# One layer of attention and mLSTM on one core: the first weight block is rounded by VectorE, and the products of zeros around the first transposes are set anew

## What is computed

```
h = rms_norm(x, pre_norm_g[l])
proj = jnp.einsum('bsd,dc->bsc', h, w_in[l])
aq, ak, av, az, mq, mk, mv, mo, mz, mi, mf = split_columns(proj)
...
y = jnp.einsum('bsc,cd->bsd', jnp.concatenate([ya, ym], axis=-1), w_out[l])
x = x + rms_norm(y, post_norm_g[l])
```

## Time and profile before

| | |
|---|---|
| median of 3 runs | 326.0 us (325.98 to 326.64) |
| the profiled execution, its own time | 326.21 us |
| its span, first to last instruction | 324.1 us |
| TensorE busy | 316.8 us, 98% of the span |
| VectorE, ScalarE, GpSimd busy | 224.6, 167.2, 88.4 us |
| granted TensorE clock, mean | 0.995 |

### The profile page before, as it was taken

The page is one execution under the profiler, slowest core; times in us unless marked ns, Lnnn a source line. Parts: engine busy times, 40 slices in busy tenths (PEclk is TensorE's granted clock), DMA queues, the critical chain, the costliest instruction groups (busy, mean ns, idle before and its releaser), DMA issues.

```text
span 324.1 us, 5056 instructions
## 1 busy us (share of the span) xinstructions
PE 316.8 (98%) x1638; PEld 262.0 (81%) x1638; DVE 224.6 (69%) x533; ACT 167.2 (52%) x335; POOL 88.4 (27%) x113
## 2 busy tenths in 40 slices
PE   7999999999999999999999999999999999999993
PEld 5887788888888888888888888778888888888882
DVE  2444999857998579976897557675477776765534
ACT  3538662598345434664257442375556976442211
POOL 8101002205440222002220025591721975001000
PEclk9999999999999999999999999999999999999998
DMA  7931553843735581145823332210120366010111
GB/s 222 303 85 48 135 168 81 157 141 97 137 73 137 136 168 36 32 133 135 138 66 103 93 97 68 77 58 31 60 70 2 119 198 270 2 65 2 65 65 65
DMA packets 27016, 33.51 MB, mean 103 GB/s; under 512 B 3768, under 2 KB 15328, under 8 KB 26992
## 3 DMA queue, kind: packets, MB, share of 16 engines
q1 hardware_dynamic: 25712, 30.38, 32.3%
q0 software_dynamic: 1120, 2.68, 6.2%
q10 hardware_dynamic: 160, 0.14, 0.1%
HBM read 31.06 MB, written 2.13 MB: 102 GB/s over the span
## 4 chain that ended last, share of the span: by engine, by line
PE 94%; issue 3%; DVE 1%; DVEq 0%; ACT 0%; POOLq 0%; POOL 0%; ACTq 0%
PE bank L1443 24%; PE bank L1445 24%; PE bank L1444 23%; PE bank L1490 4%; PE bank L1793 3%; PE bank L1740 3%; PE bank L1761 3%; PE bank L1578 2%; PE bank L1471 1%; PE bank L1458 1%; PE bank L1691 1%; PE bank L1751 1%; PE bank L1579 1%; PE bank L1515 1%; PE bank L1516 1%
## 5 line engine op out<-in xcount | busy, mean ns | idle before, releaser
L1443 PE MATMUL bank<-w_hi,xT_hi 128*128 128x512 f32 (+1 forms) x244 | 98.2, 402 | 0.0
L1445 PE MATMUL bank<-w_hi,xT_lo 128*128 128x512 f32 (+1 forms) x244 | 94.9, 389 | 0.0
L1444 PE MATMUL bank<-w_lo,xT_hi 128*128 128x512 f32 (+1 forms) x244 | 94.3, 387 | 0.0
L729 ACT ACTIVATE w_hi<-w_raw 128x512 fp32r<-128x512 f32 x72 | 44.0, 625 | 55.8 <-PE bank L1445 55.8
L1445 PEld LDWEIGHTS bank<-w_hi,xT_lo 128*128 128x128 f32 x244 | 45.8, 188 | 9.8
L1443 PEld LDWEIGHTS bank<-w_hi,xT_hi 128*128 128x128 f32 x244 | 46.0, 188 | 7.9 <-issue 0.4
L1444 PEld LDWEIGHTS bank<-w_lo,xT_hi 128*128 128x128 f32 x244 | 46.0, 189 | 7.6
L977 DVE TENSOR_TENSOR w_lo<-w_raw,w_hi 128x512 fp32r<-128x512 f32 x64 | 45.0, 718 | 5.0 <-ACT w_hi L729 4.5
L905 ACT ACTIVATE rarena<-bank 128x512 fp32r<-128x512 f32 (+3 forms) x32 | 13.9, 436 | 24.6 <-PE bank L1793 24.5
L1316 DVE CUSTOM_DVE_ANT_0 farena<-bank,causal 128x512 f32<-128x512 f32 (+3 forms) x32 | 15.5, 484 | 14.9 <-PE bank L1740 14.9
L1443 PE MATMUL bank<-xT_hi,w_hi 128*128 128x512 f32 x64 | 25.7, 402 | 0.0
(11 more groups left out here) (214 smaller groups left out, 596.3 us busy)
## 6 DMA issues: line engine op xcount, KB each, us to landing
w_raw<-in_w_in SPq DMA_DIRECT2D x72, 256.0 KB, 2.9
w_raw<-in_w_out SPq DMA_DIRECT2D x16, 256.0 KB, 2.7
gy<-in_x SPq DMA_DIRECT2D x4, 512.0 KB, 7.2
out_y<-gy SPq DMA_DIRECT2D x7, 256.0 KB, 2.0
farena<-in_x SPq DMA_DIRECT2D x4, 256.0 KB, 4.6
farena<-in_x SPq DMA_DIRECT2D x2, 512.0 KB, 6.6
farena<-g_rows POOLq DMA_DIRECT2D x4, 256.0 KB, 3.9
farena<-g_rows POOLq DMA_DIRECT2D x4, 192.0 KB, 5.5
```

The costliest lines, as they stand in the source:

```text
L729: a.activation(w_hi[:, n % RING, :], w_raw[:, n % RAW, :], ACT.Copy).then_inc(w_hi_done, 1)
L1443: pe.matmul(o, hi, m_hi, start=start, stop=False)
L1444: pe.matmul(o, hi, m_lo, start=False, stop=False)
L1445: return pe.matmul(o, lo, m_hi, start=False, stop=stop)
```

## The change

Three things are edited. VectorE rounds weight block 0 itself, ahead of its first `x_low`, and ScalarE goes from `x_hi(0)` to block 1, once block 0 is counted. The zeros are written in two pieces, 128 columns and then 384, each with its own count on `idle_set`. And the products of zeros become two of 128 columns (when the first piece is there) and four of 512 ahead of the gains' transpose, in place of five of 512, and one behind the transposes of piece 0, in place of three.

```diff
@@ scalar
             x_hi(0)
-            cut(0)
+            a.wait_ge(w_hi_done, 1)
+            cut(1)
             x_hi(1)
-            cut(1)
             for k in range(2, NK):
@@ vector
-            v.memset(idle_in.bitcast(F32), 0.0).then_inc(idle_set, 1)
+            v.memset(idle_in[:, 0:P].bitcast(F32), 0.0).then_inc(idle_set, 1)
+            v.memset(idle_in[:, P:].bitcast(F32), 0.0).then_inc(idle_set, 1)
             v.wait_ge(par_ps, 1)
             v.tensor_copy(pcol[:, 0:R_AG], bank[6][:, 0:R_AG]).then_inc(par_done, 1)
...
+            v.wait_ge(raw_in[0], 16)
+            v.tensor_copy(w_hi[:, 0, :], w_raw[:, 0, :]).then_inc(w_hi_done, 1)
             x_low(0)
             cut(0)
@@ tensor
             pe.wait_ge(idle_set, 1)
-            keep_busy(5)
+            for _ in range(2):
+                pe.matmul(bank[7][:, 0:P], idle_in[:, 0:P], idle_in[:, 0:P], start=True, stop=True)
+            pe.wait_ge(idle_set, 2)
+            keep_busy(4)
             pe.wait_ge(ident_done, 1)
...
             turn_x(0)
-            keep_busy(3)
+            keep_busy(1)
```

## The result

The change makes the kernel slower: 328.36 us median (six executions, 327.99 to 329.11) against 326.03 us before. The ratio is 1.0074, with a 95% interval of 1.0061 to 1.0087, so 0.7% slower. Forecast were 325.5 us and a range of 324.8 to 326.6. The profiled execution took 327.99 us, its span is 326.3 us.

A forecast was written before the change was run, and what follows sets the result against it. TensorE was taken as the bound, busy 316.8 of 324.1 us, with gains only in the first 8 us. Its first real product 0.93 us earlier, before a clock rise at 7.0, gains 0.47: 325.5 us, range 324.8 to 326.6.

The forecast's parts named there:

- Part 1, the zeros: Kernel start: a shorter first memset and fewer wide products of zeros bring the gains' transpose 0.35 us earlier (0.25 to 0.43).
- Part 2, the transposes: Transposes of x's piece 0 follow at 3.80, x having landed at 3.7; ScalarE's rounding of x ends at 5.65.
- Part 3, block 0: VectorE rounds weight block 0 from 4.9 in 0.42 us; first real product starts at 5.73, 0.93 us earlier.
- The rival "held up": VectorE's rounding waits for GpSimd's memset and runs 6.15 to 6.57; no gain, 326.0 us; chance 0.1.
- the rise comes later: TensorE idles 0.6 us before its first real product, clock rises at 11.2 instead of 7.0: 327.6 us; chance 0.15.
- C: Experimenters' theory: the clock's late rise comes from what TensorE does, or doesn't, ahead of the first real products.
- The sum's own case: First real product 0.93 us earlier, clock still rising at 7.0: gain 0.47 us, 325.5 us; chance 0.5.
- the sum's term of a rise at 7.0: TensorE's clock rises at 7.0 us as before, so the 0.93 us earlier start gains 0.47 us.
- the clock rises sooner: TensorE's earlier work brings the clock up before 5.73: gain 1.1 us, times 324.7 to 325.1; chance 0.25.

The follow-up runs named there:

- experiment 1: Changed kernel with GpSimd's row of memsets waiting until weight block 0 is rounded: 326.89 us, ratio 1.0007 to the kernel before.
- experiment 10: Changed kernel with GpSimd's memsets waiting until block 0 is rounded and three products of zeros behind the transposes instead of one: 325.47 us, ratio 0.9985.
- experiment 8: Changed kernel with GpSimd's row cut behind its first memset, the second waiting until block 0 is rounded: 325.92 us, ratio 0.9998.
- experiment 3: Changed kernel with six products of zeros instead of one behind the transposes of x's piece 0: 326.7 us, ratio 1.0015.
- experiment 2: Changed kernel with block 0 rounded by a two-source maximum of the block with itself instead of a copy: 325.61 us, ratio 0.9988.
- experiment 4: Kernel before with the new zeros alone, one wide product behind the transposes, ScalarE still rounding block 0: 327.62 us, ratio 1.0042.
- experiment 6: Changed kernel with block 0 rounded by a two-source operation and two products of zeros behind the transposes instead of one: 325.51 us, ratio 0.9984.
- experiment 7: Changed kernel with block 0 rounded by a two-source operation and three products of zeros behind the transposes instead of one: 325.56 us, ratio 0.9975.
- experiment 5: Kernel before with VectorE's copy rounding block 0 alone, the products of zeros left at five and three: 327.79 us, ratio 1.0047.
- experiment 9: Changed kernel with one more memset, of 1026 columns, at the head of GpSimd's row: 329.31 us, ratio 1.0099.
- experiment 12: Changed kernel with GpSimd's row of memsets waiting for the landing of block 0, as VectorE's copy does: 327.92 us, ratio 1.0043.

## Why the prediction was wrong

**Part 1, the zeros: right.** The memset of 128 columns takes 0.17 where 0.28 was taken, TensorE starts at 1.12 (1.31 forecast), and the gains' transpose comes 0.40 us earlier (0.35 forecast, bounds 0.25 and 0.43).

**Part 2, the transposes: right.** x had landed, they start at 3.76; `x_hi(0)` moves with them.

**Part 3, block 0: this is the step that failed.** The block was to land at 4.88, VectorE to start the rounding at 4.9, and: "I take 0.42". As the operation's own price 0.42 was good, experiments 1 and 10 have 0.43, with some luck: of its two ways to that number one doesn't come out, since 0.22 at 128 columns, grown as the two rows of the other operation grow (0.280 to 0.416), is 0.36. The 0.08 from x rounded to the first product has no row either; experiments 8 and 10 have 0.05. But the bounds, 0.42 and 0.69, were those of an operation undisturbed, and beside GpSimd's row it took 2.19 and 2.28, 2.96 and 3.23 us in four traces. The rival "held up" named the mechanism with its place, and was mis-sized twice. It let the copy wait for one memset, 6.57, where the row of four counts, 7.45. And it took 0.1 for its chance on the argument that the copy would be in front; the block landed at 5.2 in the trace of the change, and in experiment 3 a copy issued well in front was held as well.

The observation that was set against the rule, GpSimd's selection beginning inside a memset of VectorE, was of another kind of pair than a copy, and carried no such weight. The rule of the Trainium skill, "SBUF — State Buffer", section "SBUF: two separate sides", under the diagram of the ports, stood in the text: an fp32 copy of one source and a GpSimd operation lock each other out for a whole instruction, and who starts first has it. The runs agree with it in what is held (the copy 2.19 against 0.43, the two-source operation 0.69 beside the memsets, the memset of 6 columns 0.37 against 0.09 in turn). They differ from it in two things: the copy waited for a whole row and not for one instruction, and in experiment 3 it had started 0.67 us ahead of the first memset and was held.

**The clock: named, but as a thing apart, and out of the sum.** The rival "the rise comes later" had its chance of 0.15 and its price, 327.6, on an idle time of 0.6 us. What wasn't seen is that the two rivals belong together: a copy that is held up leaves TensorE idle for 2.3 us, and then the clock is late as well. Each of them alone would have ended at 326.7 (experiment 3) or 326.9 (most executions of experiment 1); the change had both, 328.36. The range ended at 326.6 and so left out even the price of the one rival; that of both together was never worked out.

**How sure is C?** The kernels that differ in the number of products of zeros alone say that what TensorE does there shifts how often the rise is late: with the rounding of two sources, one, two and three such products gave 5 of 12, 3 of 12 and 0 of 8 late executions; with GpSimd's row behind the copy, one and three gave 6 of 8 and 0 of 11; with ScalarE's rounding 5 of 6 and 1 of 12. One product against two is no difference that so few executions can show, and one execution with three, at 324.7, is a tenth of a microsecond short of what counts as late with one. Kernels with one product and with three also ran on different chips; on one chip stand experiments 1, 2 and 4 with one product, 16 of 26 late, and experiment 3 with six, 0 of 11. It isn't the idle time alone: experiment 3 idles 0.64 us, more than the 0.35 of experiments 1 and 2, behind six such products, and none of its eleven was late. And it isn't certain in one execution: the same program goes either way. The section "What's actually happening" of "TensorE: Matmul & The Clock Gate" in the Trainium skill has the monitor run freely beside the kernel; two groups of executions of one program are what that would look like, though no run here shows the monitor.

**The sum's own case**, a copy that isn't held and a rise near 7.0, is in none of the traces. Where the rounding wasn't held for long, the first product starts at 5.65 to 5.82 (experiments 1, 2, 8 and 10; 5.73 forecast), at 5.97 and 5.98 in experiments 6 and 7. But the clock is then late (1 and 2, near 10) or up sooner than before: in experiments 4, 6, 7, 8 and 10 the first four products take 1.00 to 1.05 us to the next row, where the kernel before takes 1.14. So the sum's term of a rise at 7.0 "as it does now" didn't hold either, and spans of 323.0 in experiments 8 and 10, 1.1 us below the 324.1 of before, are those of the rival "the clock rises sooner", which had put 1.1 on it. So the medians of 325.5 to 325.6 of experiments 6, 7 and 10, close to the forecast 325.5, don't confirm the sum: they are reached with other starts and another rise.

**Left open:** what lets a copy in. It was held to the last memset of the whole row (the change, experiments 3, 5, 9), let in ahead of the first when the row ended behind it (8), and between the first and the second when the row itself had waited (12), one trace each. Memsets alone don't explain it: the copies of experiments 3 and 8, started at 4.49 and 4.47, were not done 0.43 us later, though no memset began before 5.15. Whether GpSimd's issuing of loads, its last two from 4.06 to 5.18, is part of it wasn't tried; experiment 1 has a copy of 0.43 us, from 4.66, in the middle of it.

## What to carry to other kernels

Work moved to VectorE at a kernel's start meets what GpSimd does there, and a copy within SBUF with one source can be held for a whole row of memsets; give it two sources, if what stands beside it only writes, as a memset does (0.69 us instead of 0.43 here), or let the memsets wait for it. Price a held instruction with everything that its lateness leaves idle, the clock of TensorE above all: products of zeros that look superfluous, because nobody waits for them, may be what brings the clock up in time. And when two rivals feed each other, the range has to hold their sum.

## What the runs showed that I had not expected

That a row of GpSimd's memsets stretched a copy of 0.43 us to 2.19 and, a memset longer, to 3.23, and ended with it to 0.1 us. That six executions of eight of a kernel whose first product came 0.8 us earlier (in the one with a trace) were slower than before. And that the products of zeros ahead of the first real work shift a chance, not a time: the clock was early or late by some 2 us of span in executions of the same program.
